# Chunks of 288 and 256 tokens, with one 512-column product for the second chunk's rounded and remainder parts

## The chip, the cores and the metric

The kernel runs on one core of a Trainium2 chip. The metric is the time of one execution on the device in microseconds; a kernel's time is the median of its runs. The engines are named as in the profile: PE (TensorE, matrix products), PEld (its weight loads), DVE (VectorE), ACT (ScalarE), POOL (GpSimd) and SP (the queue that issues the loads).

## The reference, cut to what matters

One decoder layer for 544 tokens, 512 of a prompt and 32 of a sample, with 1024 features (D_FF is 2816):

```python
def ffn_half_step(x, w1, w3, w2, g, b):
    return layer_norm(ALPHA * x + 0.5 * swiglu(x, w1, w3, w2), g, b)

def swiglu(x, w1, w3, w2):
    return (jax.nn.silu(x @ w1) * (x @ w3)) @ w2

def merge_out(pool_z, attn_o, gates, w_pool_out, w_attn_out, w_out):
    g = jax.nn.sigmoid(gates.astype(jnp.float32)).astype(pool_z.dtype)
    m = g[..., 0, :] * (pool_z @ w_pool_out) + g[..., 1, :] * (attn_o @ w_attn_out)
    return m @ w_out
```

The layer is `ffn_half_step`, then h2 = LN2(ALPHA*h1 + Mixer(h1)), then a second `ffn_half_step`. The mixer projects h1 once to pool channels u, q, k, v and two gates; it pools u over trailing windows, does sliding-window attention with rotary positions and sinks, and merges both branches as above. All values are f32.

## The kernel before, in words

Features lie on the partitions and tokens along the free dimension. The 544 tokens are cut into two chunks c of C = 272 (`tok`). The weights are cut into units of 128 output columns. FFN1 and FFN2 each have two halves of 22 up units (gate and up columns in turn) and 8 down units; the mixer has 42 units (four for the pool channels u, then U_V, U_K, four U_Q, eight gate A, eight pool projections, then gate B and attention projections in turn), and w_out has 8.

Each f32 operand is split into a rounded part (`_hi`) and the remainder (`_lo`), both in the type fp32r. `part(u, c, ...)` (L1251) does one unit for one chunk: for each k-tile of 128 features (8, in the down units 11, in the projections of the branches 4) three products go into one bank of PSUM, each with its own weight load of 128 columns:

```python
pe.matmul(o, weights(s, k, True), x_hi[:, k, tok(c)], start=k == 0, stop=False)
pe.matmul(o, weights(s, k, True), x_lo[:, k, tok(c)], start=False, stop=False)
ins = pe.matmul(o, weights(s, k, False), x_hi[:, k, tok(c)], start=False, stop=k == kn - 1)
```

These are L1274 to L1276. Counted over the program there are 1392 k-tiles of weights (1056 in the FFNs, 208 in the mixer's projections of `act`, 64 in the branch projections, 64 in w_out), so 8352 products for both chunks.

Who does what beside PE: SP loads raw weights. ACT rounds them into a ring of four slots (`split`, L550), which waits for `mm_done[1]`, the products of chunk 1 three units before. DVE subtracts for the remainder (L830) once ACT has rounded, and PE's `part` waits for it (`lo_done`).

What leaves PSUM, before: in the up units ACT puts Silu of the gate unit into `tmp_a` (`through`, L599), and DVE multiplies the up unit by it (`hidden`, L842), rounds (L848) and subtracts (L850). Down units of the first half go through ACT (L599) and are added to `y` by DVE (`residual`, L855), those of the second half by DVE alone (`residual_half`, L870), w_out by `residual_out` (L862). In the mixer, `epilogue` copies u and v on ACT (L695 to L704), puts the gates through a sigmoid on ACT (L708, and L599 for gate B), rotates K and Q on DVE (`rotate`, L1051 to L1058) and multiplies projections by gates on DVE (L1077, L1083 to L1087). Attention's scores, sums and transposes run beside these units (`beside`, a table of stages); L1145 is one of its reductions, L1176 the remainder of its output, L1390 scores for the sample.

Order of the work: each engine has a fixed order, written out. PE goes through the units with chunk 1 two units behind chunk 0 (LAG = 2), in loops (`Fori`) in the middle of each half. In w_out all of chunk 0's units come before chunk 1's, in the down units of an FFN's second half most of them (DOWN_ORDER), and the norm of chunk 0 goes beside chunk 1's units. In the up units each chunk has four banks, elsewhere two. The norms: POOL sums `y` and its squares, PE spreads the sums over the partitions with f32 products (L1296 to L1310), DVE and ACT do the rest.

Of the kernel before, what the change touches and what calls it, by code (L numbers as in the profile page):

```python
# [27 lines left out]
P = 128  # L28
D = 1024
# [5 lines left out]
C = T // 2  # L35
# [95 lines left out]
def program(nc, a, out):  # L131
    ctx = ExitStack()
    with ctx:
# [7 lines left out]
        act_hi = sb("act_hi", [P, KD, T], F32R)  # L141
        act_lo = sb("act_lo", [P, KD, T], F32R)
# [15 lines left out]
        fsum = sb("fsum", [P, 2, C])  # L158
        stat = sb("stat", [P, 2, C])
        table = sb("table", [P, 3])  # L160
        p0 = sb("p0", [P, KD * C])
        tmp_a = sb("tmp_a", [P, 2, C])
        tmp_v = sb("tmp_v", [P, 2, C])
        sq = p0[:, :].rearrange("p (o t) -> p o t", o=KD)
        tmp_r, scratch = stat[:, 1, :], stat[:, 0, 0:max(WINDOWS)]
        MAX, NEG_MAX, SINK, SUM, DEN, REC = range(6)


        with ExitStack() as ffn_mem:
# [3 lines left out]
            hid_hi = sb("hid_hi", [P, KF, T], F32R, ffn_mem)  # L173
            hid_lo = sb("hid_lo", [P, KF, T], F32R, ffn_mem)
            far_hi = sb("far_hi", [P, 2, KF, P], F32R, ffn_mem)
            far_lo = sb("far_lo", [P, KF, P], F32R, ffn_mem)
        with ExitStack() as mix_mem:
# [7 lines left out]
            att_lo = sb("att_lo", [P, GQ, T], F32R, mix_mem)  # L185
            with ExitStack() as q_mem:
                qT = sb("qT", [P, GQ, T], F32, q_mem)
            att_hi = sb("att_hi", [P, GQ, T], F32R, mix_mem)
# [3 lines left out]
            with ExitStack() as branch_mem:  # L192
                pz_hi = sb("pz_hi", [P, NG, T], F32R, branch_mem)
                pz_lo = sb("pz_lo", [P, NG, T], F32R, branch_mem)
# [10 lines left out]
            m_hi = sb("m_hi", [P, KD, T], F32R, mix_mem)  # L205
            m_lo = sb("m_lo", [P, KD, T], F32R, mix_mem)
# [7 lines left out]
        for i, dead in enumerate((att_lo, att_hi)):  # L214
            flat = dead[:, :, :].rearrange("p j t -> p (j t)")
            spare[SLOTS + 2 + i] = tuple(flat[:, h * D:(h + 1) * D].rearrange("p (k n) -> p k n", k=KD) for h in range(2))
# [37 lines left out]
        uctx_done = sem("uctx_done")  # L254
        v_step = sem("v_step")
# [16 lines left out]
        def tok(c):  # L272
            return slice(c * C, c * C + C)

# [29 lines left out]
        def sq_slot(c, o):  # L304

            return 4 * c + (o if o < 4 else 1 + (o - 4) % 3)
# [25 lines left out]
        def _(sp):  # L332
# [69 lines left out]
            for c, k0, k1 in Y_PARTS:  # L402
# [4 lines left out]
                sp.dma_start(out["y"][c, :, k0:k1, :], y[:, k0:k1, tok(c)]).then_inc(stored, 16)  # L407
# [6 lines left out]
        def _(pool):  # L414
# [14 lines left out]
            def norm_sums(l, c, o):  # L429


                if 1 <= o < KD - 1:
# [9 lines left out]
                    first = y[:, 0, tok(c)] if o == 1 else fsum[:, c, :]  # L442
                    pool.tensor_tensor(fsum[:, c, :], first, y[:, o, tok(c)], ALU.add).then_inc(fsum_done[c], 1)  # L443
                for k in range(1 if o == 3 else o, o + 1) if 3 <= o < KD - 1 else ():
# [3 lines left out]
                    total = sq[:, 4 * c, :]  # L448
                    pool.tensor_tensor(total, total, sq[:, sq_slot(c, k), :], ALU.add).then_inc(sqsum_done[c], 1)
# [71 lines left out]
        def _(act):  # L521

            def split(u, kn, at=None):

                r = (u if at is None else at) % RAWS
                act.wait_ge(raw_in[r], u * (32 // RAWS) + (32 - r * (32 // RAWS)))
                s = slot = slot_of(u) if at is None else at % SLOTS
                if slot >= FAR:
                    far = slot - FAR
                    act.activation(far_hi[:, far, 0:KD, :], raw[:, r, :, :], ACT.Copy)  # L530
                    act.activation(far_hi[:, far, KD:KF, :], ext_raw[:, r, :, :], ACT.Copy).then_inc(hi_done, 1)
                    return
                if slot >= SLOTS:

                    if slot >= NEAR:
                        act.wait_ge(m_done[1], KD)
                    act.wait_ge(mm_done[1], WO_BASE)
                    act.activation(spare[slot][0], raw[:, r, :, :], ACT.Copy).then_inc(hi_done, 1)
                    return
                if at is None and 0 <= u - MIX_BASE < SLOTS:  # L540

                    act.wait_ge(mm_done[1], u - (SLOTS + 1))
                elif at is None and 0 <= u - FFN2_BASE < SLOTS:

                    act.wait_ge(mm_done[1], u - (2 * SLOTS + 1))
# [1041 lines left out]
```

## Time and profile before

| what | value |
|---|---|
| time, median of 3 runs | 1133.21 us (1132.62 to 1133.6) |
| the profiled execution's own time | 1132.04 us |
| its span, first to last instruction | 1130.3 us |
| mean granted clock of PE | 0.996 |
| PE busy | 1104.1 us (98%) |
| DVE busy | 554.7 us (49%) |
| ACT busy | 351.9 us (31%) |
| POOL busy | 130.4 us (12%) |
| HBM read, written | 97.63 MB, 3.68 MB |

The span is split by the order of the layer: FFN1 to some 430 us, the mixer with attention to some 650, w_out and its norm to some 730, FFN2 after that. A "busy" PE includes the streaming of its columns and whatever lies between back-to-back products, so a busy share of 100% doesn't say how close the stream is to its clock; that is read from the distance of the starts. Mean durations of PE rows (291 ns) contain the length of its pipeline and overlap.

### The profile page before, as it was taken

The numbers are of one execution on the slowest core, as the hardware profiler recorded it, in microseconds if no ns is written. First come the engines' busy times: TensorE is split into PE (matmuls) and PEld (weight loads), VectorE is DVE, ScalarE is ACT, GpSimd is POOL, SyncE is SP. The second block draws the span as 40 slices with busy tenths as digits, with TensorE's granted clock in tenths as the row PEclk, the third lists the DMA queues.
The fourth block names the chain that finished last, engine by engine and source line by source line (L and its number), as shares of the span: only waits on it lengthen the run. The fifth ranks groups of instructions, "written<-read, shape, count | busy, mean of one in ns | idle before, by whom it ended". The sixth has DMA issues, their size and how long they took to land.

```text
span 1130.3 us, 21492 instructions
## 1 busy us (share of the span) xinstructions
PE 1104.1 (98%) x8655; PEld 1087.1 (96%) x8655; DVE 554.7 (49%) x942; ACT 351.9 (31%) x606; POOL 130.4 (12%) x134
## 2 busy tenths in 40 slices
PE   7999999999999999999999999999999999999994
PEld 6999999999999999998899999999999999999994
DVE  4434433243344496887555576834442233444355
ACT  4222222122222234375442254321231222223223
POOL 2000000000001355700000034400000000000223
PEclk9999999999999999999999999999999999999998
DMA  7222431222232222221122350122232222223102
GB/s 258 94 93 79 150 112 57 75 94 86 81 128 97 76 98 92 85 67 38 47 94 76 104 178 18 57 94 93 82 128 75 70 75 95 84 90 126 53 2 79
DMA packets 54757, 101.12 MB, mean 89 GB/s; under 512 B 6104, under 2 KB 18712, under 8 KB 54664
## 3 DMA queue, kind: packets, MB, share of 16 engines
q1 hardware_dynamic: 53376, 95.71, 26.1%
q0 software_dynamic: 1312, 4.44, 1.2%
q8 instruction: 50, 0.82, 0.3%
q14 instruction: 19, 0.16, 0.0%
HBM read 97.63 MB, written 3.68 MB: 90 GB/s over the span
## 4 chain that ended last, share of the span: by engine, by line
PE 91%; DVE 6%; ACT 1%; issue 1%; DMA 1%; POOL 0%; SPq 0%; DVEq 0%
PE psum L1274 29%; PE psum L1276 29%; PE psum L1275 29%; DVE stat L916 1%; DVE y L911 1%; DVE y L947 1%; PE psum L1405 1%; DVE act_lo L954 1%; PE psum L1421 1%; DVE y L943 1%; DMA y<-in_x 1%; PE psum L1438 0%; ACT p L752 0%; PE psum L1310 0%; PE psum L1296 0%
## 5 line engine op out<-in xcount | busy, mean ns | idle before, releaser
L1274 PE MATMUL psum<-act_hi,ring_hi 128*128 128x272 f32 x1792 | 520.9, 291 | 8.7 <-DVE ring_lo L966 7.1
L1276 PE MATMUL psum<-act_hi,ring_lo 128*128 128x272 f32 x1792 | 520.9, 291 | 0.0
L1275 PE MATMUL psum<-act_lo,ring_hi 128*128 128x272 f32 x1792 | 517.4, 289 | 0.0
L1274 PEld LDWEIGHTS psum<-act_hi,ring_hi 128*128 128x128 f32 x1792 | 339.0, 189 | 13.7 <-DVE ring_lo L966 7.4
L1275 PEld LDWEIGHTS psum<-act_lo,ring_hi 128*128 128x128 f32 x1792 | 339.7, 190 | 0.0
L1276 PEld LDWEIGHTS psum<-act_hi,ring_lo 128*128 128x128 f32 x1792 | 338.7, 189 | 0.0
L830 DVE TENSOR_TENSOR ring_lo<-raw,ring_hi 128x1024 fp32r<-128x1024 f32 (+1 forms) x159 | 189.9, 1194 | 289.3 <-ACT ring_hi L550 248.1
L550 ACT ACTIVATE ring_hi<-raw 128x1024 fp32r<-128x1024 f32 (+1 forms) x159 | 161.0, 1013 | 238.3 <-PE psum L1276 237.2
L599 ACT ACTIVATE tmp_a<-psum 128x272 f32<-128x272 f32 x136 | 54.1, 398 | 344.6 <-PE psum L1276 316.2
L1274 PE MATMUL psum<-hid_hi,ring_hi 128*128 128x272 f32 x448 | 130.3, 291 | 0.0
L1275 PE MATMUL psum<-hid_lo,ring_hi 128*128 128x272 f32 x448 | 128.8, 288 | 0.0
L1276 PE MATMUL psum<-hid_hi,ring_lo 128*128 128x272 f32 x448 | 128.8, 287 | 0.0
L443 POOL TENSOR_TENSOR fsum<-y 128x272 f32<-128x272 f32 x6 | 6.5, 1086 | 733.9 <-DVE y L870 531.7
L1275 PEld LDWEIGHTS psum<-hid_lo,ring_hi 128*128 128x128 f32 x448 | 84.5, 189 | 0.2
L1274 PEld LDWEIGHTS psum<-hid_hi,ring_hi 128*128 128x128 f32 x448 | 84.3, 188 | 0.2
L1276 PEld LDWEIGHTS psum<-hid_hi,ring_lo 128*128 128x128 f32 x448 | 84.5, 189 | 0.0
L842 DVE TENSOR_TENSOR tmp_v<-psum,tmp_a 128x272 f32<-128x272 f32 x88 | 38.7, 440 | 78.4 <-PE psum L1276 77.9
L855 DVE SCALAR_TENSOR_TENSOR y<-y,tmp_a 128x272 f32<-128x272 f32 x32 | 14.2, 443 | 81.8 <-ACT tmp_a L599 81.8
L1275 PE MATMUL psum<-hid_lo,ext_hi 128*128 128x272 f32 x168 | 48.5, 289 | 0.0
L1274 PE MATMUL psum<-hid_hi,ext_hi 128*128 128x272 f32 x168 | 48.4, 288 | 0.0
L1276 PE MATMUL psum<-hid_hi,ext_lo 128*128 128x272 f32 x168 | 48.4, 288 | 0.0
L850 DVE TENSOR_TENSOR hid_lo<-tmp_v,hid_hi 128x272 f32 (+1 forms) x88 | 39.1, 444 | 8.7
(210 smaller groups left out, 1303.8 us busy)
## 6 DMA issues: line engine op xcount, KB each, us to landing
raw<-in_ffn_up SPq DMA_DIRECT2D x175, 256.0 KB, 2.9
raw<-in_ffn_down SPq DMA_DIRECT2D x32, 512.0 KB, 3.5
raw<-in_mix_wide SPq DMA_DIRECT2D x52, 256.0 KB, 2.9
ext_raw<-in_ffn_down SPq DMA_DIRECT2D x32, 192.0 KB, 3.5
raw<-in_mix_proj SPq DMA_DIRECT2D x32, 128.0 KB, 2.2
raw<-in_w_out SPq DMA_DIRECT2D x16, 256.0 KB, 2.9
y<-in_x SPq DMA_DIRECT2D x3, 544.0 KB, 6.9
out_y<-y SPq DMA_DIRECT2D x2, 544.0 KB, 3.0
```

The lines of the kernel that those rows point to most:

```text
L550: ins = act.activation(ring_hi[:, s, 0:n, :], raw[:, r, 0:n, :], ACT.Copy)
L599: act.activation(tmp_a[:, c, :], psum[:, bank_of(u if at is None else at, c), 0:C], func, scale=scale) \
L830: ins = dve.tensor_tensor(ring_lo[:, s, 0:n, :], raw[:, r, 0:n, :], ring_hi[:, s, 0:n, :], ALU.subtract)
L842: dve.tensor_tensor(tmp_v[:, c, :], psum[:, bank_of(at, c), 0:C], tmp_a[:, c, :], ALU.mult) \
L850: dve.tensor_tensor(lo, v, hi, ALU.subtract).then_inc(hid_done[c], 1)
L855: dve.scalar_tensor_tensor(out=y[:, o, tok(c)], in0=y[:, o, tok(c)], scalar=factor, in1=tmp_a[:, c, :], op0=ALU.mult, op1=ALU.add).then_in ...
L911: ins = dve.tensor_tensor(half, half, mean, ALU.subtract)
L916: dve.reciprocal(stat[:, c, :], stat[:, c, :]).then_inc(rec_done[c], 1)
L943: dve.tensor_tensor(pair, pair, r, ALU.mult).then_inc(norm_done[c], 1)
L1274: pe.matmul(o, weights(s, k, True), x_hi[:, k, tok(c)], start=k == 0, stop=False)
L1275: pe.matmul(o, weights(s, k, True), x_lo[:, k, tok(c)], start=False, stop=False)
L1276: ins = pe.matmul(o, weights(s, k, False), x_hi[:, k, tok(c)], start=False, stop=k == kn - 1)
```

## The change

The chunks become 288 and 256 tokens (`CN`, C0, C1). Rounded and remainder parts of an operand lie as two planes in one tensor (`act`, `hid`, `pz`, `att`, `mix`), so that one product can read both planes of chunk 1: 2 x 256 columns, which fill a bank of 512. For chunk 0 each k-tile has the three products as before, with 288 columns. For chunk 1 it has two: `wide` (rounded weights by both planes, 512 columns) and `low` (remainder of the weights by the rounded plane, 256 columns, into one half of the bank). The result of chunk 1 is then the sum of the bank's halves, and DVE forms it with `summed`, a reduction over pairs (L874), or by a second residual step. ACT's Silu and sigmoid for chunk 1 no longer read PSUM but what DVE has summed (`silu`, L631, and L731), and the copies of u and v for chunk 1 move from ACT to DVE. The inputs and outputs x and y become two arrays each.

The core of the diff:

```diff
-C = T // 2
+CN = (288, 256)
+C0, C1 = CN
+HALF = T // 2
...
-        act_hi = sb("act_hi", [P, KD, T], F32R)
-        act_lo = sb("act_lo", [P, KD, T], F32R)
+        act = sb("act", [P, 2, KD, T], F32R)
+        act_hi, act_lo = act[:, 0], act[:, 1]
...
+        def both(bank, lo=0, hi=C1):
+            return psum[:, bank, :].rearrange("p (a t) -> p t a", a=2)[:, lo:hi, :]
...
+            def silu(u, n):
+
+                sc.wait_ge(evac[1], u + 1)
+                if not isinstance(n, int) or n:
+
+                    sc.wait_ge(prod_done, n)
+                sc.activation(tmp_a[:, 1, 0:C1], pair[:, 0, :], ACT.Silu).then_inc(silu_done, 1)
...
                         if s % 2 == 0 and s >= LAG:
-                            through(u - LAG, 1, ACT.Silu, at=b + s - LAG)
+                            silu(u - LAG, n - 1)
                         if kn:
                             split(u + 2, kn, at=b + s + 2)
...
+                if c:
+                    if U_GA <= m < U_PA or m >= U_GB and not is_proj(m):
+                        dst = m1[:, m - U_GA, tok(1)] if m < U_PA else tmp_a[:, 1, 0:C1]
+                        sc.wait_ge(evac[1], u + 1)
+                        if m > U_GB:
+
+                            sc.wait_ge(m_done[1], (m - U_GB) // 2)
+                        sc.activation(dst, tmp_v[:, 1, 0:C1], ACT.Sigmoid).then_inc(gate_done, 1)
...
+            def summed(u, dst, at=None):
+
+                dve.wait_ge(mm_done[1], u + 1)
+                dve.wait_ge(evac[1], u)
+                return dve.tensor_reduce(dst, both(bank_of(u if at is None else at, 1)), AX.X, ALU.add)
+
+            def gate_up(u, at):
+
+                summed(u, pair[:, 0, :], at).then_inc(evac[1], 1)
...
+                if c:
+                    summed(u, v, at).then_inc(evac[1], 1)
+                    dve.wait_ge(evac[1], u + 1)
+                    dve.wait_ge(silu_done, n + 1)
+                    dve.tensor_tensor(v, v, tmp_a[:, 1, 0:C1], ALU.mult).then_inc(prod_done, 1)
...
+                ins = dve.scalar_tensor_tensor(out=row, in0=out_of(bank_of(u, c), c), scalar=0.5, in1=row,
+                                               op0=ALU.mult, op1=ALU.add)
+                if c:
+                    step(ins)
+                    ins = dve.scalar_tensor_tensor(out=row, in0=halves(bank_of(u, 1))[1], scalar=0.5, in1=row,
+                                                   op0=ALU.mult, op1=ALU.add)
+                ins.then_inc(evac[c], 1)
...
+                        if s % 2 == 0 and s >= LAG:
+                            gate_up(u - LAG, b + s - LAG)
...
+                elif c and m == U_V:
+                    summed(u, vT[:, tok(1)]).then_inc(evac[1], 1)
+                elif c and (U_GA <= m < U_PA or m >= U_GB and not is_proj(m)):
+                    if m > U_GA:
+
+                        dve.wait_ge(gate_done, m - U_GA if m < U_PA else KD + (m - U_GB) // 2)
+                    if m > U_GB:
+                        dve.wait_ge(m_done[1], (m - U_GB) // 2)
+                    summed(u, tmp_v[:, 1, 0:C1]).then_inc(evac[1], 1)
...
-                    o = psum[:, bank, 0:C]
-                    pe.matmul(o, weights(s, k, True), x_hi[:, k, tok(c)], start=k == 0, stop=False)
-                    pe.matmul(o, weights(s, k, True), x_lo[:, k, tok(c)], start=False, stop=False)
-                    ins = pe.matmul(o, weights(s, k, False), x_hi[:, k, tok(c)], start=False, stop=k == kn - 1)
+                    if c:
+                        low = (halves(bank)[order[0]], weights(s, k, False), x[:, order[0], k, tok(1)])
+                        wide = (psum[:, bank, :].rearrange("p (a t) -> p a t", a=2), weights(s, k, True), x[:, :, k, tok(1)])
+                        if k < kn - 1:
+                            pe.matmul(*wide, start=k == 0, stop=False)
+                            pe.matmul(*low, start=False, stop=False)
+                        else:
+                            pe.matmul(*low, start=False, stop=False)
+                            ins = pe.matmul(*wide, start=False, stop=True)
+                    else:
+                        o, hi, lo = out_of(bank, 0), x[:, order[0], k, tok(0)], x[:, order[1], k, tok(0)]
+                        pe.matmul(o, weights(s, k, True), hi, start=k == 0, stop=False)
+                        pe.matmul(o, weights(s, k, True), lo, start=False, stop=False)
+                        ins = pe.matmul(o, weights(s, k, False), hi, start=False, stop=k == kn - 1)
```

In the order of PE, at a place in the mixer where the units change from the pool projection (`pz`) to the attention projection (`att`), both with four k-tiles; the rows of before are the last k-tile of the one and the first of the next:

```order
L1274 MATMUL psum<-pz_hi,ring_hi 128x272
L1275 MATMUL psum<-pz_lo,ring_hi 128x272
L1276 MATMUL psum<-pz_hi,ring_lo 128x272
L1274 MATMUL psum<-att_hi,ring_hi 128x272
L1275 MATMUL psum<-att_lo,ring_hi 128x272
L1276 MATMUL psum<-att_hi,ring_lo 128x272
```

And with the change, the end of a unit of chunk 1, then the first rows of the next unit's chunk 0:

```order
L1378 MATMUL psum<-pz,ring_hi 128x512
L1379 MATMUL psum<-pz,ring_lo 128x256
L1381 MATMUL psum<-pz,ring_lo 128x256
L1382 MATMUL psum<-pz,ring_hi 128x512
L1385 MATMUL psum<-att,ring_hi 128x288
L1386 MATMUL psum<-att,ring_hi 128x288
L1387 MATMUL psum<-att,ring_lo 128x288
```

Three products of 272 columns have become, for chunk 1, one of 512 and one of 256, the last k-tile in the reverse order; chunk 0 has three of 288. All other rows of PE keep their places.

In the order of ACT with its waits, in the gate B rounds. `m_done` counts merged units, `evac1` banks of chunk 1 that have been read. Before:

```order
L599 ACTIVATE tmp_a<-psum 128x272 [waits evac0,mm_done0]
L599 ACTIVATE tmp_a<-psum 128x272 [waits evac1,mm_done1]
L550 ACTIVATE ring_hi<-raw 128x1024 [waits mm_done1,raw_in0]
L550 ACTIVATE ring_hi<-raw 128x512 [waits mm_done1,raw_in1]
L599 ACTIVATE tmp_a<-psum 128x272 [waits evac0,mm_done0]
L599 ACTIVATE tmp_a<-psum 128x272 [waits evac1,mm_done1]
```

With the change:

```order
L623 ACTIVATE tmp_a<-psum 128x288 [waits evac0,mm_done0]
L731 ACTIVATE tmp_a<-tmp_v 128x256 [waits m_done1,evac1]
L571 ACTIVATE ring_hi<-raw 128x1024 [waits mm_done1,raw_in0]
L571 ACTIVATE ring_hi<-raw 128x512 [waits mm_done1,raw_in1]
L623 ACTIVATE tmp_a<-psum 128x288 [waits evac0,mm_done0]
L731 ACTIVATE tmp_a<-tmp_v 128x256 [waits m_done1,evac1]
```

Chunk 1's gate (second row) waited for PE and now waits for DVE, and the two roundings of weights stand behind it as before.

In the order of DVE with its waits, at the start of an FFN half, ahead of the loop. `hi_done` counts ACT's rounded weights, `mm_done0` and `mm_done1` PE's units of each chunk, `hid_done0` finished hidden rows; ISA and REGISTER_ALU rows only carry waits and addresses. Before:

```order
L830 TENSOR_TENSOR ring_lo<-raw,ring_hi 128x1024 [waits hi_done]
L837 REGISTER_ALU
L838 REGISTER_ALU [waits mm_done0]
L841 ISA [waits evac0]
L842 TENSOR_TENSOR tmp_v<-psum,tmp_a 128x272 [waits hid_done0]
```

With the change:

```order
L874 TENSOR_REDUCE pair<-psum 128x256 [waits evac1,mm_done1]
L844 REGISTER_ALU
L865 TENSOR_TENSOR ring_lo<-raw,ring_hi 128x1024 [waits hi_done]
L885 ISA
L893 REGISTER_ALU [waits hid_done0]
L894 REGISTER_ALU [waits mm_done0]
L895 TENSOR_TENSOR tmp_v<-psum,tmp_a 128x288 [waits evac0]
```

The sum of the gate unit (L874) has come ahead of the remainder of the weights (L865, before L830) that PE waits for.

## Rows read from the trace of the kernel before

**Rows 1.** The page, part 1: busy us, share of the span, instructions.

```profile
PE 1104.1 (98%) x8655; PEld 1087.1 (96%) x8655; DVE 554.7 (49%) x942; ACT 351.9 (31%) x606; POOL 130.4 (12%) x134
```

**Rows 2.** The page, part 4: the chain that ended last, by engine.

```profile
PE 91%; DVE 6%; ACT 1%; issue 1%; DMA 1%; POOL 0%; SPq 0%; DVEq 0%
```

**Rows 3.** Stretches in FFN1: from:to, length, PE, PEld, DVE, ACT, POOL, clock, DMA.

```profile
100.00:200.00 100.00, 100.00 (x801) 100.00 (x800) 36.60 (x62) 25.09 (x42) 1.56 (x3) 1.00 0.32 107
200.00:300.00 100.00, 100.00 (x797) 100.00 (x796) 36.73 (x61) 23.00 (x34) 0.00 (x0) 1.00 0.25 81
```

**Rows 4.** Timeline (start us, us, engine, line) of PE and its loads.

```profile
300.00 0.29 PE L1276 MATMUL psum<-act_hi,ring_lo 128*128 128x272 f32 x1
300.01 0.19 PEld L1274 LDWEIGHTS psum<-act_hi,ring_hi 128*128 128x128 f32 x1
300.13 0.29 PE L1274 MATMUL psum<-act_hi,ring_hi 128*128 128x272 f32 x1
...
300.25 0.29 PE L1275 MATMUL psum<-act_lo,ring_hi 128*128 128x272 f32 x1
```

**Rows 5.** Timeline of PE near the start of the kernel.

```profile
8.84 0.43 PE L1276 MATMUL psum<-act_hi,ring_lo 128*128 128x272 f32 x1
9.07 0.43 PE L1274 MATMUL psum<-act_hi,ring_hi 128*128 128x272 f32 x1
```

**Rows 6.** Timeline of PE, f32 products of a norm.

```profile
391.77 0.62 PE L1306 MATMUL psum<-p,mean_w 128*128 128x272 f32 x2
392.23 0.62 PE L1308 MATMUL psum<-y,mean_w 128*128 128x272 f32 x2
```

**Rows 7.** Groups of DVE by form: shapes, count | busy us, mean ns | idle.

```profile
L842 DVE TENSOR_TENSOR tmp_v<-psum,tmp_a 128x272 f32<-128x272 f32 x88 | 38.7, 440 | 78.4 <-PE psum L1276 77.9 <-ACT tmp_a L599 0.6
...
L1176 DVE TENSOR_TENSOR att_lo<-psum,att_hi 128x512 fp32r<-128x512 f32 x4 | 2.8, 692 | 0.1
...
L1145 DVE TENSOR_REDUCE soft<-p 128x8 f32<-128x1024 f32 x1 | 1.2, 1220 | 0.0
```

**Rows 8.** Timeline of all engines, first FFN, start of a half.

```profile
27.41 1.05 ACT L550 ACTIVATE ring_hi<-raw 128x1024 fp32r<-128x1024 f32 x1
...
28.50 1.23 DVE L830 TENSOR_TENSOR ring_lo<-raw,ring_hi 128x1024 fp32r<-128x1024 f32 x1 [8.27 <-ACT ring_hi L550]
...
29.93 0.29 PE L1274 MATMUL psum<-act_hi,ring_hi 128*128 128x272 f32 x1
```

**Rows 9.** Timeline of all engines, one gate B round.

```profile
604.97 0.40 ACT L599 ACTIVATE tmp_a<-psum 128x272 f32<-128x272 f32 x1 [2.61 <-PE psum L1276]
...
606.35 1.23 DVE L830 TENSOR_TENSOR ring_lo<-raw,ring_hi 128x1024 fp32r<-128x1024 f32 x1 [3.93 <-ACT ring_hi L550]
...
607.79 0.29 PE L1274 MATMUL psum<-act_hi,ring_hi 128*128 128x272 f32 x1
```

**Rows 10.** Stretches of 20 us, norm 1 and attention.

```profile
410.00:430.00 20.00, 19.68 (x144) 18.61 (x142) 18.41 (x31) 8.59 (x17) 7.25 (x11) 1.00 0.48 161
...
450.00:470.00 20.00, 20.00 (x162) 19.99 (x162) 17.63 (x34) 4.10 (x6) 19.83 (x18) 1.00 0.25 80
470.00:490.00 20.00, 20.00 (x157) 19.31 (x156) 19.23 (x40) 9.25 (x13) 2.78 (x5) 1.00 0.26 82
490.00:510.00 20.00, 19.92 (x159) 19.13 (x159) 15.53 (x34) 18.15 (x48) 0.00 (x0) 1.00 0.18 52
```

**Rows 11.** Waits of PE: line, what for, us in total, times, longest.

```profile
PE psum L1274 <- DVE y L870: 2.5, 3, 1.6
...
PE psum L1390 <- DVE att_lo L1176: 0.8, 1, 0.8
```

**Rows 12.** Timeline of PE, a product with idle time behind it.

```profile
429.57 0.29 PE L1276 MATMUL psum<-act_hi,ring_lo 128*128 128x272 f32 x1
430.05 0.39 PE L1274 MATMUL psum<-act_hi,ring_hi 128*128 128x272 f32 x1 [0.18 <-DVE act_lo L954]
```

More of the change, by code:

```diff
@@ L701, in epilogue @@
                 elif m == U_V:
[L702 to L704 removed]
+                    sc.wait_ge(mm_done[0], u + 1)
+                    sc.wait_ge(evac[0], u)
+                    sc.activation(vT[:, tok(0)], out_of(bank, 0), ACT.Copy).then_inc(evac[0], 1)
                 elif U_GA <= m < U_PA:
[L706 removed]
@@ L707, in epilogue @@
-                    act.wait_ge(evac[c], u)
-                    act.activation(m1[:, m - U_GA, tok(c)], psum[:, bank, 0:C], ACT.Sigmoid).then_inc(evac[c], 1)
+                    sc.wait_ge(mm_done[0], u + 1)
+                    sc.wait_ge(evac[0], u)
+                    sc.activation(m1[:, m - U_GA, tok(0)], out_of(bank, 0), ACT.Sigmoid).then_inc(evac[0], 1)
                 elif m >= U_GB and not is_proj(m):
-                    through(u, c, ACT.Sigmoid)
+                    through(u, 0, ACT.Sigmoid)
@@ L773, in _ @@
                     for g in range(NG):
-                        act.activation(segs[:, g, :, 0:BUF], rows[:, g], ACT.Copy).then_inc(uctx_done, 1)
+                        sc.activation(segs[:, g, :, 0:BUF], rows[:, g], ACT.Copy).then_inc(uctx_done, 1)
                 beside(s - 0.5)
@@ L1324, in up_static @@
                             ready = None if c else first_ready
-                        part(b + s, c, KD, act_hi, act_lo, ready=ready)
+                        part(b + s, c, KD, act, ready=ready)
                     up_static(0, 0)
@@ L1445, in mix_part @@
                 if not is_proj(m):
-                    part(u, c, KD, act_hi, act_lo, ready=act_wait(1, c) if m == 0 else None)
+                    part(u, c, KD, act, ready=act_wait(1, c) if m == 0 else None)
                 elif m < U_GB:
@@ L1455, in mix_part @@
                         pe.wait_ge(att_free, freed("PVs" if c else "PV2"))
-                    part(u, c, NG, att_hi, att_lo)
+                    part(u, c, NG, att, order=lo_first)
             def beside(at):
@@ L1524, in span @@
         return np.arange(o * P, (o + 1) * P)
-    arrays = {"x": np.stack([features(tokens[c * C:(c + 1) * C]) for c in range(2)])}
+    arrays = {"x0": features(tokens[0:C0]), "x1": features(tokens[C0:T])}
     for l in ("ffn1", "ffn2"):
@@ L1562, in results @@
 def results(r):
-    y = np.concatenate([r["y"][c].transpose(2, 1, 0).reshape(C, D) for c in range(2)])
+    y = np.concatenate([r[f"y{c}"].transpose(2, 1, 0).reshape(CN[c], D) for c in range(2)])
     u = r["pool_u_new"].transpose(2, 1, 0).reshape(BUF + NS, POOLW)
```

352 lines of the change are left out of this document (196 added, 156 removed).

## The prediction

> **What bounds the kernel now.** I read the page's first part, then the chain, the stretches, the timeline of PE, and last DVE's groups. PE is busy 1104.1 of 1130.3 us, DVE 554.7 [rows 1]; the chain that ended last is 91% PE and 6% DVE [rows 2]. So the end is the sum of the products plus the few places where PE waits. In the FFN stretches 100 to 200 and 200 to 300 us PE never stops (100.00 of 100) and starts 801 and 797 products: 200 us by 1598 is 125.2 ns a product [rows 3]. The granted clock is 1.00 there, the level of 2.4 GHz, at which 272 columns stream in 272/2.4 = 113.3 ns. So each product takes some 11.9 ns more than its columns; the 8352 products make 99 us of that. On the timeline the starts of PE's rows stand 0.12 to 0.13 us apart [rows 4]. The extra is not everywhere: near the start of the kernel, at the 1.2 GHz level, the starts are 0.23 apart, and 272/1.2 is 226.7 [rows 5]; and the f32 products of the norms take two records in 0.46 us, 0.229 each, which is two cycles a column (226.7) and 2.3 ns [rows 6].
>
> **What the change does to PE.** For one k-tile of both chunks there were six products of 272 columns (1632); now there are three of 288, one of 512 and one of 256, again 1632 columns. One product and one weight load fall away per k-tile, and no column. There are 1392 k-tiles: 1056 in the FFNs, 208 in the mixer's projections from `act`, 64 in the branch projections, 64 in w_out. What one product less saves is not shown by the trace, since every rounded product there has 272 columns. Ends: 2.3 ns, the surplus of the nearest product of another kind [rows 6], if the other 9.6 ns belong to the columns; and 34.8 ns, if the weight load is what spaces the products (rival 2). I take 11.9 ns, the whole surplus, as a price paid once per product: starts with equal columns still scatter between 0.12 and 0.13 [rows 4], which looks like something done at each start rather than a steady rate. That makes 1392 x 11.9 ns = **-16.6 us**.
>
> The Trainium skill, page "TensorE: Matmul & The Clock Gate", section "Back-to-back issue gap", speaks against this: its warm gap is columns/2.4 plus 2.5 ns, so that a product less would give 2.5 ns and 1392 of them 3.5 us, an estimate from that page. The f32 rows agree with it (2.3 ns), the rounded ones do not (11.9 ns) [rows 4, 6].
>
> **What the change puts on DVE and ACT.** Chunk 1's two halves must be added before anything uses them, and a sum reads 512 values from the bank. The reduction L1145 takes 1220 ns for 1024 values; a two-input operation takes 692 for 512 and 440 for 272 [rows 7]. I take 0.69 us for a sum of 512. 138 new sums make 95 us, and 40 second residual steps of 0.43 us another 17, which takes DVE to some 660 us: not the bound in all, but each place counts for itself.
>
> *FFN, steady loop.* Two sums more per 12 us; DVE is busy 36.7 of 100 us there [rows 3]. The 63 us of idle time hide them: 0. If that cover were gone it would cost 1.4 us for each pair of units.
>
> *FFN, start of each half.* There the rounding of weights (L550) stands on ACT behind chunk 1's first Silu, and the remainder (L830) on DVE behind L550. ACT rounds from 27.41 to 28.46, DVE subtracts from 28.50 to 29.73, and PE takes the unit up at 29.93: 0.20 us in hand [rows 8]. Now the Silu waits for the sum (0.69) and two hand-offs between engines (0.04 each, by the step from 28.46 to 28.50), and chunk 1's part is some 0.25 us shorter, which brings the next need forward. 0.69 + 0.08 + 0.25 - 0.20 = 0.82, and with DVE's queue ahead of the sum some 0.9 us, four times (two halves of two FFNs): **+3.6 us**.
>
> *Mixer, gate B rounds.* The same chain: gate at 604.97, remainder from 606.35 to 607.58, needed at 607.79, 0.2 us in hand [rows 9]. The sum now stands before the sigmoid, and two epilogues stand before it on DVE; by the same sum I take 0.8 us for each of the seven rounds: **+5.6 us**.
>
> *Mixer, attention.* From 450 to 510 us DVE is busy 17.63, 19.23 and 15.53 of 20 [rows 10], idle 7.6 us in all. V, K, four Q and eight gate A units each get a sum, ten of them in that stretch: 6.9 us. The idle time is not free to take, since DVE works in a fixed order and is idle where it waits for PE and ACT; the rotations and scores queued behind a sum come later, and PE waits for them as it already does once, 0.8 us at L1390 for what DVE left in L1176 [rows 11]. A gate further passes through one buffer to ACT, so that DVE's next sum waits for the sigmoid (0.40 as L599's [rows 9]). 14 x 0.69 + 8 x 0.40 = 12.9: **+13 us**. Lower end 0 (all in idle time), upper end the 30 sums from V to the last gate B, 20.7 us.
>
> *w_out and the norms.* Chunk 1's residual is two steps on DVE instead of one. Sixteen of the extra ones (0.43 us each, 6.9 us) lie before the first two norms, where the window from 410 us shows DVE at 18.41 of 20 [rows 10] and PE already waits 2.5 us for y [rows 11]. I take **+6 us** (0 to 6.9), and **+1 us** for the last norm, behind which nothing runs (two residual steps, and operations on 288 columns).
>
> *At nothing:* planes in one tensor, two input tensors for one, their loads and stores: the same bytes in the same order on SP's queue, hidden by PE's stream. The group products keep 272 columns.
>
> Sum against the profiled execution's own 1132.04 us: 1132.0 - 16.6 + 3.6 + 5.6 + 13 + 6 + 1 = **1144.6, say 1145 us**. The median of the runs, 1133.21, is 0.1% above that execution, which I leave in the rounding. With attention at its ends this case runs from 1132 to 1153.
>
> **The rivals.**
> 1. *The surplus goes with the columns*: a rounded column streams at 2.17 a ns instead of 2.4. For it: a stream half as fast, by f32 or by the clock, shows no surplus or little [rows 5, 6], as a limited supply of operands would. Against it: the scatter of the starts. Then 2.3 x 1392 = 3.2 us come back and the waits stay: 1132.0 - 3.2 + 29.2 = **1158 us**. The skill's section named above comes to the same for what a product less is worth.
> 2. *The weight load spaces the products.* In the steady stretch the next load starts with each product [rows 4], and where PE streams longer, by f32 or at 1.2 GHz, the surplus is gone or small [rows 5, 6]. Then any product up to 288 columns takes 125.2, the wide one 512/2.4 + 2.3 = 215.6, a k-tile 716.4 instead of 751.2 ns: -48.4 us and 1132.0 - 48.4 + 29.2 = 1112.8, say **1113 us**, the other side. It decides as soon as it saves over 21 ns a k-tile (29.2 us by 1392). Against it: a product with none behind it, at 429.57 before PE idles to 430.05, is recorded at 0.29 us as all others [rows 12], so its own stream is stretched.
> 3. *The waits find idle time.* PE gains as forecast, and only the half starts and gate rounds remain: 1132.0 - 16.6 + 9.2 = 1124.6, say **1125 us**. For it: DVE is busy only 49% [rows 1]. Against it: 450 to 490 us has 3.1 us of idle time [rows 10] for seven sums of 4.8.
>
> That the change doesn't do what it says is excluded by PE's order: one row of 512 and one of 256 per k-tile.
>
> **How the numbers follow.** Forecast 0.42, rival 1 0.24, rival 2 0.14, rival 3 0.14, other 0.06. About 0.2% (2.3 us) is what a measurement of this kernel can tell from no change. Slower: 0.40 of the forecast, 0.22 of rival 1, 0.03 of others, 0.65. Faster: 0.13 of rival 2, 0.12 of rival 3, 0.03 of others, 0.28. Within: 0.07, from the edges where attention costs nothing. The range reaches from rival 2's 1113 to 1162, which is rival 1 with attention half-way to its upper end; the forecast's own is 1132 to 1153.
>
> **What would show it.** Right: starts 132 ns apart for 288 columns (120 + 11.9), 225 for 512, 119 for 256, in sum 740 instead of 751 a k-tile; PE idle 20 to 40 us more than before, most of it between 440 and 590 us, behind DVE's sums; some 0.9 us of it behind the remainder (now L865) at each half start. Wrong: 133 for 288 and 236 for 512 (rival 1); 125 for 288 and 216 for 512 (rival 2); PE idle no more than 10 us above before (rival 3).

## The result and the profile after

| | before | with the change |
|---|---|---|
| time, median of 4 runs | 1133.4 us (1132.62 to 1133.89) | 1159.72 us (1158.78 to 1162.6) |
| ratio to before | | 1.0242 (95%: 1.0229 to 1.0255) |
| span of the profiled execution | 1130.3 us | 1156.9 us |
| mean granted clock | 0.996 | 0.989 |

The change makes the kernel 26.3 us slower; the span grows by 26.6. The direction is the one forecast (1145), the size is more than twice it. First the page of the changed kernel, busy times and the chain (as [rows 1, 2] of before):

```profile
PE 1105.5 (96%) x7263; PEld 1021.7 (88%) x7263; DVE 658.1 (57%) x1120; ACT 355.3 (31%) x593; POOL 128.0 (11%) x134
...
PE 76%; DVE 17%; ACT 3%; issue 3%; DMA 0%; DVEq 0%; POOL 0%; SPq 0%; ACTq 0%
```

PE has 1392 instructions fewer, as the change says, but is not a microsecond less busy (1104.1 before): busy time includes streaming and whatever lies between products, so this alone suggests that a product less has been worth little. DVE's share of the chain went from 6 to 17%: 11 points more of the span's chain now run through DVE. The waits of PE (which line, for what, us in total, times, longest):

```profile
PE psum L1385 <- DVE ring_lo L865: 10.4, 14, 1.3
PE psum L1385 <- DVE ring_lo L1032: 7.5, 2, 5.9
PE psum L1378 <- DVE y L936: 6.3, 5, 2.7
PE psum L1532 <- DVE p L1265: 3.6, 1, 3.6
PE psum L1385 <- DVE y L920: 3.1, 1, 3.1
PE psum L1407 <- POOL fsum L464: 2.5, 1, 2.5
```

With the eight smaller rows of that view they are 38.4 us in 35 waits; before there were 13.2 us in 14 ([rows 11] are two of its six rows). So 25.2 us of new waits, and the first row, the remainder of the weights, was not in the list before at all. L1032 is the start of the kernel, where 7.1 us were waited for L966 before.

**How the products fare.** In this view (groups of PE by line and form: shapes, count, busy us, mean ns) a duration is the distance of the starts plus a fixed part: before, the page had 289 ns for L1275 where the starts were 125.2 apart [rows 3], so some 163 ns.

```profile
L1378 PE MATMUL psum<-act,ring_hi 128*128 128x512 f32 x784 | 278.5, 393 | 0.4 <-DVE act L1020 0.4
...
L1386 PE MATMUL psum<-act,ring_hi 128*128 128x288 f32 x896 | 265.7, 296 | 0.0
...
L1379 PE MATMUL psum<-act,ring_lo 128*128 128x256 f32 x784 | 219.5, 280 | 0.0
```

That makes 230, 133 and 117 ns. Taken from the starts themselves (mean over all back-to-back pairs at the 2.4 GHz level), with what is left after columns/2.4:

| columns | `act`: start to start, surplus | `hid`: start to start, surplus |
|---|---|---|
| 256 | 117.2, 10.6 ns | 117.6, 10.9 ns |
| 272 (before) | 125.8, 12.4 | 125.0, 11.7 |
| 288 | 133.4, 13.4 | 133.1, 13.1 |
| 512 | 230.9, 17.6 | 232.4, 19.1 |

The surplus grows with the columns, faster from 256 to 288 than from there to 512. A k-tile of both chunks took 6 x 125.8 = 754.8 ns and takes 3 x 133.4 + 230.9 + 117.2 = 748.3 for `act`, 750.0 and 749.2 for `hid`. By the counts (912 and 352 k-tiles, and 128 others at 5 ns) that is 6.5 x 912 + 0.8 x 352 + 5 x 128 ns = 6.8 us, where 16.6 were forecast.

**The stages.** From the first product of a stage to the first of the next, in us, worked out from the traces (`e2`, `e3`, `e8` are experiments below):

```
                    before   after     e2     e3     e8
FFN1 half 1, up     138.91  136.04  137.02  139.91  136.76
FFN1 half 1, down    65.99   65.94   65.94   66.16   65.94
FFN1 half 2, up     132.89  132.79  131.70  133.22  131.70
FFN1 half 2, down    70.19   72.63   72.62   71.38   71.38
mixer to gate B     175.89  186.43  186.35  175.47  175.91
gate B rounds        67.94   72.76   67.17   67.72   67.17
w_out                52.08   59.77   54.66   52.92   54.06
FFN2 half 1, up     135.96  136.42  134.88  135.00  133.56
FFN2 half 1, down    65.99   65.94   65.94   66.16   65.94
FFN2 half 2, up     132.89  132.80  131.70  133.22  131.70
FFN2 half 2 to end   85.80   89.56   89.44   86.64   88.29
```

The FFN's long stages are level or a little faster; the loss is 10.5 us in the attention part of the mixer, 4.8 in the gate rounds, 7.7 at w_out and 6.2 around the first and the last norm.

**A new wait, followed.** Timeline of the changed kernel at the start of a half (the place of [rows 8]), all engines:

```profile
25.00 0.69 DVE L874 TENSOR_REDUCE pair<-psum 128x256 f32<-128x512 f32 x1 [5.68 <-PE psum L1382]
25.81 0.42 ACT L631 ACTIVATE tmp_a<-pair 128x256 f32<-128x256 f32 x1 [6.30 <-DVE pair L874]
26.14 1.04 ACT L571 ACTIVATE ring_hi<-raw 128x1024 fp32r<-128x1024 f32 x1
27.21 1.23 DVE L865 TENSOR_TENSOR ring_lo<-raw,ring_hi 128x1024 fp32r<-128x1024 f32 x1 [1.52 <-ACT ring_hi L571]
27.36 0.39 PE L1382 MATMUL psum<-act,ring_hi 128*128 128x512 f32 x1
...
28.49 0.40 PE L1385 MATMUL psum<-act,ring_hi 128*128 128x288 f32 x1 [0.74 <-DVE ring_lo L865]
```

The chain reads downwards: the sum (0.69), the Silu that waits for it, the rounding that has nothing to do with either and stands behind the Silu on ACT, the remainder, PE. DVE is idle 1.52 us in the middle of it. From PE's last start at 27.36 to the next at 28.49 are 1.13 us, where a product of 512 takes 0.23: 0.90 us lost, with 0.9 forecast. The row calls it 0.74, since the recorded length of a product hides some 0.17 of a wait. A gate B round shows the same end of the chain (place of [rows 9]):

```profile
618.03 1.23 DVE L865 TENSOR_TENSOR ring_lo<-raw,ring_hi 128x1024 fp32r<-128x1024 f32 x1 [1.43 <-ACT ring_hi L571]
618.31 0.40 PE L1382 MATMUL psum<-att,ring_hi 128*128 128x512 f32 x1
...
619.31 0.40 PE L1385 MATMUL psum<-act,ring_hi 128*128 128x288 f32 x1 [0.60 <-DVE ring_lo L865]
```

Here 1.00 - 0.23 = 0.77 us are lost, in each of five rounds, and 0.66 in a sixth; 0.8 was forecast for each of seven.

**The clock.** Stretches of the changed kernel (from:to, length, PE busy and starts, PEld, DVE, ACT, POOL, granted clock, DMA):

```profile
505.00:511.00 6.00, 2.36 (x18) 1.99 (x17) 3.87 (x13) 5.83 (x16) 0.00 (x0) 1.00 0.14 45
511.30:514.60 3.30, 3.30 (x16) 3.30 (x15) 0.00 (x0) 3.27 (x8) 0.00 (x0) 0.50 0.00 0
```

PE had been idle for 3.6 us (the fourth wait above), and then for 3.4 us the granted clock is 0.50, the 1.2 GHz level, with products of 288 columns 0.24 us apart. The trace has four such drops, at 511, 682, 716 and 1132 us, each behind a wait of 2.5 to 3.6 us or at its end; before there was none until the end of the work. Each costs up to 3.4 x (1 - 133/240) = 1.5 us. The stage times above contain them: one lies in the mixer up to gate B, two in w_out, one in the last stage.

### The profile page after: what moved, and what is told of

The parts are those of the page before. It is cut to its first block, busy times and chain, and to the rows that moved or that the text cites. A ratio compares the mean times of both kernels' runs of the same rounds, so it can differ in the third digit from the quotient of the medians.

```text
span 1156.9 us, 19015 instructions
## 1 busy us (share of the span) xinstructions
PE 1105.5 (96%) x7263; PEld 1021.7 (88%) x7263; DVE 658.1 (57%) x1120; ACT 355.3 (31%) x593; POOL 128.0 (11%) x134
## 4 chain that ended last, share of the span: by engine, by line
PE 76%; DVE 17%; ACT 3%; issue 3%; DMA 0%; DVEq 0%; POOL 0%; SPq 0%; ACTq 0%
PE psum L1378 19%; PE psum L1385 14%; PE psum L1387 14%; PE psum L1386 14%; PE psum L1379 10%; DVE ring_lo L865 3%; PE psum L1382 2%; ACT ring_hi L571 1%; PE psum L1381 1%; DVE stat L1127 1%; DVE y L977 1%; DVE y L1013 1%; DVE stat L982 1%; DVE tmp_v L874 1%; DVE act L1020 1%
## 5 line engine op out<-in xcount | busy, mean ns | idle before, releaser
L1385 PE MATMUL psum<-act,ring_hi 128*128 128x288 f32 x896 | 268.6, 300 | 17.3 <-DVE ring_lo L865 9.2
L1378 PE MATMUL psum<-act,ring_hi 128*128 128x512 f32 x784 | 278.5, 393 | 0.4 <-DVE act L1020 0.4
L1386 PE MATMUL psum<-act,ring_hi 128*128 128x288 f32 x896 | 265.7, 296 | 0.0
L1387 PE MATMUL psum<-act,ring_lo 128*128 128x288 f32 x896 | 265.1, 296 | 0.0
L865 DVE TENSOR_TENSOR ring_lo<-raw,ring_hi 128x1024 fp32r<-128x1024 f32 (+1 forms) x159 | 190.1, 1196 | 111.4 <-ACT ring_hi L571 89.4
L1379 PE MATMUL psum<-act,ring_lo 128*128 128x256 f32 x784 | 219.5, 280 | 0.0
L1385 PEld LDWEIGHTS psum<-act,ring_hi 128*128 128x128 f32 x896 | 169.2, 189 | 22.2 <-DVE ring_lo L865 12.6
L1378 PEld LDWEIGHTS psum<-act,ring_hi 128*128 128x128 f32 x784 | 147.1, 188 | 31.9 <-issue 2.0
L1386 PEld LDWEIGHTS psum<-act,ring_hi 128*128 128x128 f32 x896 | 169.5, 189 | 3.5
L1387 PEld LDWEIGHTS psum<-act,ring_lo 128*128 128x128 f32 x896 | 169.9, 190 | 0.0
L1379 PEld LDWEIGHTS psum<-act,ring_lo 128*128 128x128 f32 x784 | 147.4, 188 | 0.6
L874 DVE TENSOR_REDUCE pair<-psum 128x256 f32<-128x512 f32 x44 | 30.4, 691 | 114.4 <-PE psum L1382 114.4
L874 DVE TENSOR_REDUCE tmp_v<-psum 128x256 f32<-128x512 f32 x76 | 52.4, 689 | 64.4 <-PE psum L1382 64.3
L1378 PE MATMUL psum<-hid,ring_hi 128*128 128x512 f32 x224 | 80.7, 399 | 0.9 <-DVE y L936 0.9
L1385 PE MATMUL psum<-hid,ring_hi 128*128 128x288 f32 x224 | 66.5, 297 | 0.0
L1387 PE MATMUL psum<-hid,ring_lo 128*128 128x288 f32 x224 | 66.1, 295 | 0.0
L1386 PE MATMUL psum<-hid,ring_hi 128*128 128x288 f32 x224 | 66.1, 295 | 0.0
L631 ACT ACTIVATE tmp_a<-pair 128x256 f32<-128x256 f32 x44 | 18.4, 418 | 144.9 <-DVE pair L874 144.9
L1379 PE MATMUL psum<-hid,ring_lo 128*128 128x256 f32 x224 | 62.8, 280 | 0.0
```

The lines of the kernel that those rows point to most:

```text
L631: sc.activation(tmp_a[:, 1, 0:C1], pair[:, 0, :], ACT.Silu).then_inc(silu_done, 1)
L865: ins = dve.tensor_tensor(ring_lo[:, s, 0:n, :], raw[:, r, 0:n, :], ring_hi[:, s, 0:n, :], ALU.subtract)
L874: return dve.tensor_reduce(dst, both(bank_of(u if at is None else at, 1)), AX.X, ALU.add)
L1378: pe.matmul(*wide, start=k == 0, stop=False)
L1379: pe.matmul(*low, start=False, stop=False)
L1385: pe.matmul(o, weights(s, k, True), hi, start=k == 0, stop=False)
```

## The experiments

Times are medians; the ratio is to the kernel before on the same chip, whose median there was 1131.9 to 1132.3 us.

| run | time | ratio (95%) |
|---|---|---|
| e1 | 1169.11 us | 1.0331 (1.0311 to 1.0350) |
| e2 | 1146.32 | 1.0135 (1.0117 to 1.0152) |
| e3 | 1135.72 | 1.0038 (1.0024 to 1.0052) |
| e4 | 1137.38 | 1.0056 (1.0038 to 1.0074) |
| e5 | 1144.61 | 1.0111 (1.0095 to 1.0126) |
| e6 | 1140.20 | 1.0068 (1.0052 to 1.0083) |
| e7 | 1140.10 | 1.0067 (1.0051 to 1.0082) |
| e8 | 1129.39 | 0.9975 (0.9966 to 0.9985) |
| e9 | 1141.25 | 1.0072 (1.0057 to 1.0088) |
| e10 | 1131.52 | 0.9995 (0.9985 to 1.0005) |
| e11 | 1129.75 | 0.9976 (0.9966 to 0.9986) |

**e1, the wide product taken apart** (what is a product less worth):

```diff
-                        wide = (psum[:, bank, :].rearrange("p (a t) -> p a t", a=2), weights(s, k, True), x[:, :, k, tok(1)])
+                        wide = [(halves(bank)[p], weights(s, k, True), x[:, p, k, tok(1)]) for p in range(2)]
...
-                            pe.matmul(*wide, start=k == 0, stop=False)
+                            for p, w in enumerate(wide):
+                                pe.matmul(*w, start=k == 0 and p == 0, stop=False)
...
```

> The changed kernel with the 512-column product taken apart into two of 256 (one weight load more per k-tile, same banks, same sums on DVE). Theory A, the surplus goes with the columns: two starts of 117.3 ns instead of one of 231.5, 3.1 ns by 1392 k-tiles, +4.3 us on the changed kernel: about 1164 us. Theory B, a price of 11.9 ns per product as predicted: +16.6 us, about 1176 us. Theory C, the weight load spaces the products: 125 ns for each, +25 us, about 1185 us.

By the ratios the run is 0.9% (10 us) above the changed kernel, between both theories. The starts tell why: the 256-column products now stand 118.8 ns apart in `act` (117.5 in `hid`), so a chunk-1 k-tile takes 356.4 ns instead of 348.1, and 352.5 instead of 350.0. That is 8.3 and 2.5 ns for one product and its weight load less, 8.8 us in all; theory A had put it at 3.1 and theory B at 11.9. How it divides between the product and the load, this run doesn't show, since both go together. Of the stages, the second up half shows it bare: 134.07 against 132.80 us.

**e2, the rounding ahead of Silu and of the gate B sigmoid** (does the chain make the waits):

```diff
                         if s % 2 == 0 and s >= LAG:
+                            if kn:
+                                split(u + 2, kn, at=b + s + 2)
+                                kn = 0
                             silu(u - LAG, n - 1)
```

and the same in the mixer's loop for the gate B units.

> The changed kernel with the rounding of the next weights put ahead of chunk 1's Silu and gate B sigmoid on ACT; nothing else moves. Theory A, the chain sum, Silu, rounding, remainder makes the waits at the half starts (0.90, 0.99, 1.41, 0.99 us) and in six gate B rounds (0.66 and five of 0.77): all but a rest of some 1 us goes, about -8 us, 1152 us. Rival: DVE's own queue (the sum ahead of the remainder) makes them, then ACT's order changes nothing: 1159 to 1160 us.

12 us come back by the ratios where 8 were expected. Waits of PE in e2:

```profile
PE psum L1392 <- DVE ring_lo L872: 3.1, 4, 1.3
...
PE psum L1392 <- DVE y L927: 0.8, 1, 0.8
```

The remainder falls from 10.4 us in 14 waits to 3.1 in 4; the half starts and the gate rounds have no wait left (67.17 us for the gate rounds, below the 67.94 of before). The rest is a second effect: the wait of 3.1 us at the start of w_out (L920, above) shrinks to 0.8, since it was the gate rounds' delay handed on, and the clock drops at 682 and 716 us are gone. The wait behind which the second of them stood is not: L1414, which is L1407 of the changed kernel, waits 2.5 us for POOL in e2 as before. So a wait of that length can pass with a drop or without one, and w_out's 5.1 us are 2.2 of wait and some 3 of clock. All the sums are still there.

**e3, three products and no sums, with the chunks of 288 and 256**, and **e4, the wide product in the FFNs alone**:

```diff
-                    if c:
+                    if c and is_wide(u if at is None else at):
                         low = (halves(bank)[order[0]], weights(s, k, False), x[:, order[0], k, tok(1)])
```

with `is_wide` false everywhere in e3 and true in the FFNs alone in e4, and the evacuation of before wherever it is false, as here in the mixer:

```diff
-                if c:
-                    x = tmp_a[:, 1, 0:C1]
-                    step(summed(u, x))
```

> Chunks of 288 and 256 tokens, but three products for both chunks everywhere, no 512-column product, no sums, evacuation as in the kernel before. Theory A and B alike: 3 x 133.2 + 3 x 117.3 = 751.5 ns a k-tile against 751.2 before, the waits of before: 1133 us, within 3. Rival, the unequal chunks cost by themselves (longer norm of chunk 0, less cover by chunk 1): 1138 us or more; then only 21 us of the loss belong to the sums.

> The 512-column product and the sums in the FFNs only; mixer and w_out with three products of 256 for chunk 1, evacuated as before. Theory A, the loss sits in the mixer and w_out (23 of 26.6 us by the stages of both traces) and in the last norm: 1135 to 1138 us. Rival, the FFN's sums cost by keeping DVE busier all along: 1145 us or more.

e3 is within theory A's 3 us, but clear of no change: the unequal chunks cost 4 us by themselves, which the forecast had at 1: the stages give 1.2 before the first norm, 0.8 at w_out, 0.8 at the end, and up halves of 133.22 against 132.89. e4 is within its range; with the FFN's sums in place the loss of the mixer and of w_out is gone. So, taken away in this order, 1.9% of the 2.4% come from the mixer and w_out, 0.2 from the FFNs (their gain on PE counted in), 0.4 from the chunks. e3 also shows what the wide product gives where nothing waits, by the starts in 100 us of FFN1; first e3 (six products a k-tile), then the changed kernel (five):

```profile
100.00:200.00 100.00, 100.00 (x796) 100.00 (x796) 36.80 (x62) 24.69 (x41) 1.57 (x3) 1.00 0.31 102
```

```profile
100.00:200.00 100.00, 100.00 (x672) 94.35 (x671) 43.47 (x73) 26.24 (x42) 1.58 (x3) 1.00 0.32 105
```

796/6 = 132.7 k-tiles against 672/5 = 134.4, and 801/6 = 133.5 in the kernel before [rows 3]. The second number of the rows is PEld: the loads no longer fill the time, and the products hardly gain.

**e5 and e6, which sums the attention part pays for.** From here on `is_wide` reads a table by place; both runs stand on e2, e5 with chunk 1 of u, V, K and Q plain, e6 with that of gate A:

```diff
-WIDE = dict(up=True, down=True, last=True, out=True, early=True, gate=True, late=True)
+WIDE = dict(up=True, down=True, last=True, out=True, early=False, gate=True, late=True)
```

```diff
-WIDE = dict(up=True, down=True, last=True, out=True, early=True, gate=True, late=True)
+WIDE = dict(up=True, down=True, last=True, out=True, early=True, gate=False, late=True)
```

> As e2 (roundings first), but chunk 1's units for u, V, K and Q are three products of 256 evacuated as before, so that ten of the sums ahead of the softmax are gone; gate A keeps its sums. Theory A, these sums push the softmax on DVE back and PE waits for its first transposes (3.6 us idle in e2 at 506 us) and for a late remainder before (1.3 us at 483): some 5 us of the attention stage's 9 go, 1141 us. Rival, the gate A hand-off through one buffer does it: 1145 to 1146 us as e2.

> As e2, but only the eight gate A units of chunk 1 are evacuated as before (sigmoid on ACT straight from the bank); u, V, K and Q keep their sums. Theory A: the 3.6 us before the first transposes stay, what goes is the smaller waits from 520 to 550 us, some 1.5 to 2.5 us: 1144 us. Rival (gate A's hand-off): 5 us or more go, 1141 us or less.

I had this the wrong way round. Without the ten early sums the mixer up to gate B takes 183.3 us instead of 186.35; without the eight sums of gate A 179.7. In e6 this stage also has no clock drop, which is some 1.5 us of its 6.7; in e2 and e5 it has one, at 511 and 507 us. The timeline of e2 shows what gate A does:

```profile
504.33 0.68 DVE L881 TENSOR_REDUCE tmp_v<-psum 128x256 f32<-128x512 f32 x1
505.05 0.42 ACT L734 ACTIVATE m<-tmp_v 128x256 f32<-128x256 f32 x1 [5.44 <-DVE tmp_v L881]
505.37 1.04 ACT L571 ACTIVATE ring_hi<-raw 128x1024 fp32r<-128x1024 f32 x1
506.45 1.23 DVE L872 TENSOR_TENSOR ring_lo<-raw,ring_hi 128x1024 fp32r<-128x1024 f32 x1 [1.43 <-ACT ring_hi L571]
...
508.03 1.66 DVE L1272 TENSOR_SCALAR p<-p,soft 128x128 f32<-128x128 f32 x8
```

ACT stands idle 5.44 us behind a sum that is queued on DVE behind the softmax; the rounding, ready long before, stands behind that sigmoid; then DVE waits 1.43 us for the rounding, and the division that PE's first transposes need (L1272) comes last. It is the chain of the half starts again. **e9** moves the rounding ahead of gate A's sigmoid as well, with all sums in place:

```diff
-                    late = s - LAG >= U_GB and not is_proj(s - LAG)
+                    late = s - LAG >= U_GA and not is_proj(s - LAG)
```

> As e2, with the rounding of weights put ahead of the sigmoid for chunk 1's gate A too; all sums stay. Theory A, in e2 the rounding stood 1.4 us too late before the first transposes because it waits on ACT behind a sigmoid that waits for a sum queued behind the softmax on DVE; then PE's 3.6 us there shrink to some 2.2 and the attention stage as a whole gives 1.5 to 4 us: 1142 to 1145 us. Rival, only the length of the sums counts: 1146 us as e2.

The mixer up to gate B falls to 180.1 us, nearly as far as without gate A's sums, and PE's idle time before the transposes from 3.6 to 2.1 us:

```profile
PE psum L1562 <- DVE p L1295: 2.1, 1, 2.1
```

So with ACT's order alone (e2 and e9) 1.7% of the 2.4% come back, and every sum is still made. Clock is part of that: the drop in the mixer is gone in e9, some 1.5 us of the 6.2. What a drop costs, w_out shows: behind the same waits of 0.8 and 2.5 us it takes 56.21 us in e9, which has a drop there at 703 us, and 54.66 in e2, which has none.

**e7, the units in front of the norms in one step** (on e2, w_out and the second-half down units plain):

```diff
-WIDE = dict(up=True, down=True, last=True, out=True, early=True, gate=True, late=True)
+WIDE = dict(up=True, down=True, last=False, out=False, early=True, gate=True, late=True)
```

> As e2, but the down units of each FFN's second half and w_out (the units in front of the three norms) are evacuated in one step as before. Theory A, the second residual steps cost what the stages show between e2 and e3: 1.2 before the first norm, 1.7 at w_out, 2.8 at the end, some 5.7 us: 1140 to 1141 us. Rival, the unequal chunks alone set these stages: 1145 to 1146 us.

As expected in time: 1.2 us before the first norm (71.40), 0.6 at w_out (54.08), 1.3 in the first up half of FFN2 (133.57), 2.6 at the end (86.84). But of the 2.6 at the end some 1.5 are clock: e2 has a drop there at 1118 us and e7 none, behind waits of 2.7 and 2.3 us. In e8 below, with the same steps at the end and a drop at 1104 us, that stage takes 88.29.

**e10, the kernel before with its tensors moved by 96 bytes** (does the surplus hang on addresses):

```diff
+        sb("pad", [P, 24])
         act_hi = sb("act_hi", [P, KD, T], F32R)
```

> The kernel before with 96 bytes left free ahead of all tensors in SBUF, nothing else. Theory A, the surplus of a rounded product goes with its columns wherever the operand lies: starts 125.2 ns apart as before, 1132 to 1133 us. Rival, it hangs on the address of the operand (256 columns from `hid` start 115 to 117 ns apart and from `act` 119 to 120 in e1 and e3): 1 ns in the starts is 8 us, so over 3 us in either direction.

```profile
100.00:200.00 100.00, 100.00 (x801) 100.00 (x799) 35.88 (x60) 25.07 (x42) 1.57 (x3) 1.00 0.32 106
200.00:300.00 100.00, 100.00 (x797) 100.00 (x796) 36.81 (x61) 22.99 (x34) 0.00 (x0) 1.00 0.26 85
```

The same 801 and 797 starts as [rows 3], and the same time. This shift doesn't matter; why `act` and `hid` differ by 1 ns at 256 columns (118.8 against 117.5 in e1) stays open.

**e8 and e11, the wide product only where its sum is covered** (e8: FFN up units and first-half down units, pool projections, gate B, attention projections; e11 without the mixer, where ACT has the order of before again; both with the rounding ahead of Silu; e8's table, and the entry that e11 changes in it):

```diff
-WIDE = dict(up=True, down=True, last=True, out=True, early=True, gate=True, late=True)
+WIDE = dict(up=True, down=True, last=False, out=False, early=False, gate=False, late=True)
```

```diff
-WIDE = dict(up=True, down=True, last=False, out=False, early=False, gate=False, late=True)
+WIDE = dict(up=True, down=True, last=False, out=False, early=False, gate=False, late=False)
```

> The 512-column product only where its sum is covered: up units and first-half down units of the FFNs, pool projections, gate B and attention projections; roundings first on ACT. u, V, K, Q, gate A, w_out and the second-half down units with three products of 256. By the stages of e2 and e3: 1128 to 1130 us, 2 to 4 us below the kernel before. Rival, mixing both forms brings new waits where they meet: 1133 us or more.

> The 512-column product only in the FFN's up units and first-half down units, rounding ahead of Silu on ACT; mixer, w_out and second-half down units with three products of 256. By the stages of e3 and e8: 0.5 us more in the gate rounds, 1.1 less at w_out, 0.4 less in the pool projections than e8: 1128 to 1129 us. Rival, the gate rounds with sums are worth more than w_out loses: 1130 us or more.

Both are 0.25% (some 2.8 us) faster than the kernel before, the only ones that are, and not to be told apart; e11 is 0.75 us above its range. The page of e8, and the waits of PE in it:

```profile
PE 1100.4 (98%) x7647; PEld 1040.1 (92%) x7647; DVE 638.2 (57%) x1070; ACT 357.4 (32%) x606; POOL 130.7 (12%) x134
```

```profile
PE psum L1408 <- DVE ring_lo L1051: 7.2, 2, 5.9
PE psum L1408 <- DVE y L955: 3.9, 3, 2.2
...
PE psum L1524 <- DVE att L1300: 1.0, 1, 1.0
```

DVE is at 638.2 us, nearly as busy as in the changed kernel (658.1), at 30 us less time, and the waits are nearly those of before (start of the kernel, `y` before the first and the last norm, L1524 which is L1390 of before; 15.0 us in all against 13.2): the amount of DVE's work alone did not make the loss. Where it stood did, as e2 and e9 show.

## Why the prediction was right or wrong

*The price of a product less failed.* The step "I take 11.9 ns, the whole surplus, as a price paid once per product" put 16.6 us on PE's side; the starts in the changed trace give 6.8 us. I had chosen it by the scatter of starts between 0.12 and 0.13, which says nothing of how the surplus depends on columns. The better sign stood in [rows 5, 6] and I had used it only for rival 1: a stream half as fast has hardly a surplus. Measured, one product and its load less give 8.3 ns in `act` and 2.5 in `hid`, 8.8 us in all (e1), so that two thirds of the 12.4 ns in `act` are indeed a price per product (or its load), but only a fifth of the 11.7 in `hid`. The unequal chunks take some 2 us back: in e3, with six products, a k-tile takes 756.0 ns in `act` and 752.4 in `hid`, against 754.8 and 750.0 before. Neither my price nor rival 1's 2.3 ns is it. This is 10 of the 14.5 us that the forecast misses. The rule of the Trainium skill that I weighed ("TensorE: Matmul & The Clock Gate", section "Back-to-back issue gap": columns/2.4 plus 2.5 ns, given there for a product by itself) does not give these starts either: for 512 columns it would be 215.8 ns, an estimate from that page, and they are 230.9 to 232.4 apart. Its consequence, that a product less is worth 2.5 ns, is met in `hid` and missed in `act`.

*The sum of the waits came out, 29.2 us forecast and 28.8 measured, but in part by luck, since its parts did not.* The views of waits give 38.4 - 13.2 = 25.2, and 21 more waits hide some 0.17 us each, 3.6. By place: half starts 0.90 + 0.99 + 1.41 + 0.99 = 4.3 (forecast 3.6), as the chain in the prediction had it. Gate rounds 5.6 between after and e2 (forecast 5.6), of which 4.5 are the six waits followed above. Attention 11.0 between after and e3 (forecast 13), 1.5 of it a clock drop, and for another reason: the prediction counted sums by their length, and e9 shows that 6.2 of the 11, the drop among them, go when only ACT's order changes. Before the norms and at the end 1.3 + 6.9 + 2.9 (forecast 6 + 1), some 4.5 of it three clock drops; at w_out the wait itself was the gate rounds' delay handed on (e2). Of the 2.5 us for `y` that the prediction put before the first two norms, 1.6 lie before the last one, where 1 us was forecast and 2.9 came. The sign that most of PE's new idle time would lie between 440 and 590 us did not come: the waits there are 9.7 us against 0.8 before, some 9 of the 25.2.

*What was not in the sum:* the unequal chunks (4 us by e3, part of the places above, forecast inside the 1 us at the end), and the clock: four drops of up to 1.5 us each, up to 6 us; no term of the prediction held them. Against that the first rise to the 2.4 GHz level came at 9.5 us in this execution instead of 15.6, which gave back some 3 us in the first up half; it varies from kernel to kernel (9.0 to 17.0 in these runs), and I give no cause. 28.8 - 6.8 + 6 - 3 = 25.0 of the 26.6 us that the span grew.

*The rivals.* Rival 1 (surplus with the columns, 1158 us) had nearly the time and half the mechanism: the surplus grows with the columns, but less than in proportion (17.6 ns at 512 against 10.6 at 256; 512 columns stand 231 apart, between the forecast's 225 and the rival's 236). The time is luck: it gives back 3.2 us where 6.8 came, and lacks the net 3 us that the clock cost. Rival 2 (the weight load sets a spacing of 125 ns) is refuted: loads fell from 8655 to 7263 and 1392 of them gave 6.8 us instead of 48, and with a load each the 256-column products stand 117 ns apart and those of 288 columns 133. Rival 3 (waits in idle time) is refuted by the waits. FFN's steady loop at nothing was right: 132.79 us against 132.89, the wait at the half's start included, with DVE busier.

## What to carry to other kernels

When a step on one engine gets a new producer, look at what stands behind it in its queue: here an unrelated rounding of weights stood behind the Silu, and moving it one place up was worth 1.7% of the time, with the clock drops that went, while the sums themselves were nearly free where PE had no need of DVE soon. Price a removed instruction from rows that differ in the quantity that changes (columns against count); if there are none, a bound is not a value, and the sum is to be shown at both bounds (2.3 and 34.8 ns here, where 4.9 came). A wait of 2 to 4 us can also cost clock, some 1.5 us here, and not every such wait does: where PE is the bound, count it in as a range.

## What the runs showed of the hardware that was not expected

Rounded (fp32r) products at the 2.4 GHz level carry a surplus of 10.6, 12.4, 13.4 and 17.6 ns at 256, 272, 288 and 512 columns of `act`, and none at the 1.2 GHz level (288 columns 0.24 us apart, 288/1.2 = 240 ns). What makes it is open; an address shift of 96 bytes doesn't (e10), and one product with its weight load less per k-tile takes 2.5 to 8.3 ns off it (e1). Nor is it set by the columns alone: the 256-column products of `act` have 10.6 ns beside a wide one and 12.1 where all six are apart (e1). The granted clock fell to 0.50 for 3.4 us behind waits of 2.5 to 3.6 us in a kernel that is 96% busy on PE. The length of the wait doesn't settle it: e8 has a drop behind one of 2.2 us at 1102 us, and there is none behind 2.5 us at 704 in e2 nor right behind 3.6 us at 504 in e7.
